# Reordering the opening of a decoder block: first tiles and first normalisation rows loaded in halves on both queues, first two value tiles multiplied in passes

## What is computed

```python
h = layer_norm(x, ln0_g, ln0_b)                 # per token, over 1024 features
proj = jnp.einsum('bsd,dn->bsn', h, w_in[i])     # 1024 x 7688 columns
(hg_q, hg_f, hg_i, hg_g, fx_q, ...) = jnp.split(proj, split_at, axis=-1)
...
v = i_lin.astype(jnp.float32)                    # hg_i, the values of the first mixer: 512 columns
```

## Time and profile before

| what | value |
|---|---|
| median of 3 runs | 1638.04 us (1636.09 to 1638.63) |
| the profiled execution's own time | 1637.65 us |
| its span, first to last instruction | 1635.8 us (1.85 us lie around it) |
| TensorE busy in the span | 1588.1 us, 97% |
| first transpose, first matmul of a product | 13.3 us, 17.99 us |
| second value tile's product done, third begins | 33.8 us |
| eight value tiles done | 71.2 us |

### The profile page before, as it was taken

One profiled execution on the slowest core, in us unless ns is written; L12 is line 12 of the kernel. 1 busy time (PEld: TensorE's weight loads), 2 busy tenths in 40 slices (PEclk: granted clock), 3 DMA queues, 4 the chain that ended last, 5 costly groups with the idle time before them and its releaser, 6 DMA issues.

```text
span 1635.8 us, 21111 instructions
## 1 busy us (share of the span) xinstructions
PE 1588.1 (97%) x7800; PEld 1325.1 (81%) x7800; DVE 1150.4 (70%) x1724; ACT 744.0 (45%) x1162; POOL 694.2 (42%) x487
## 2 busy tenths in 40 slices
PE   6999999999999999999999989999999999999996
PEld 4888888888888887888887868888888888888886
DVE  8558878437767668656336879986666579857977
ACT  3245454327888774511233644445444553433342
POOL 5222221522333145564443597765566323223334
PEclk9999999999999999999999999999999999999999
DMA  8211110101010143521333435554444598867672
GB/s 295 77 42 38 27 39 27 39 29 38 27 53 27 39 117 97 147 78 52 122 120 118 164 126 183 182 195 143 159 168 152 185 330 254 272 199 238 194 204 104
DMA packets 220693, 208.51 MB, mean 127 GB/s; under 512 B 9000, under 2 KB 190504, under 8 KB 218544
## 3 DMA queue, kind: packets, MB, share of 16 engines
q1 hardware_dynamic: 217424, 196.09, 38.7%
q10 hardware_dynamic: 3168, 11.08, 1.7%
HBM read 160.96 MB, written 46.17 MB: 127 GB/s over the span
## 4 chain that ended last, share of the span: by engine, by line
PE 83%; DVE 5%; ACT 4%; DMA 2%; POOL 2%; issue 2%; SPq 0%; DVEq 0%; ACTq 0%; POOLq 0%
PE dense L969 7%; PE dense L971 7%; PE dense L973 7%; PE dense L979 4%; PE dense L1315 3%; PE dense L1317 3%; PE dense L1316 3%; PE dense L1395 3%; PE dense L1396 3%; PE dense L1397 3%; PE mixA L1106 2%; PE dense L1047 2%; PE dense L1049 2%; PE dense L1048 2%; PE mixA L1315 2%
## 5 line engine op out<-in xcount | busy, mean ns | idle before, releaser
L969 PE MATMUL dense<-parts 128*128 128x512 f32 x528 | 183.3, 409 | 1.6 <-DVE page L2090 0.9
L943 POOL TENSOR_TENSOR parts<-page,parts 128x512 fp32r<-128x512 f32 x52 | 88.9, 1733 | 208.1 <-ACT parts L1909 208.1
L862 POOL TENSOR_TENSOR parts<-page,parts 128x512 fp32r<-128x512 f32 x108 | 156.3, 1469 | 44.9 <-ACT parts L1788 41.6
L971 PE MATMUL dense<-parts 128*128 128x512 f32 x528 | 174.0, 391 | 0.0
L973 PE MATMUL dense<-parts 128*128 128x512 f32 x528 | 173.3, 390 | 0.0
L854 POOL CAST parts<-page 128x1024 fp32r<-128x1024 f32 x43 | 49.3, 1145 | 287.4 <-PE dense L973 192.4
L905 POOL TENSOR_TENSOR page<-page 128x512 f32<-128x512 f32 x80 | 122.6, 1532 | 59.8 <-PE dense L1317 25.2
L913 POOL TENSOR_TENSOR parts<-page,parts 128x512 fp32r<-128x512 f32 x80 | 114.8, 1437 | 55.4 <-ACT parts L1835 50.6
L1919 ACT CAST parts<-page 128x1024 fp32r<-128x1024 f32 x56 | 58.8, 1055 | 142.8 <-DVE page L2614 123.2
L973 PEld LDWEIGHTS dense<-parts 128*128 128x128 f32 x528 | 99.1, 188 | 21.8
L971 PEld LDWEIGHTS dense<-parts 128*128 128x128 f32 x528 | 99.1, 188 | 21.0
(11 more groups left out here) (298 smaller groups left out, 4315.8 us busy)
## 6 DMA issues: line engine op xcount, KB each, us to landing
page<-in_w_ff SPq DMA_DIRECT2D x104, 512.0 KB, 6.0
page<-in_w_in SPq DMA_DIRECT2D x120, 256.0 KB, 3.2
page<-act_scratch SPq DMA_DIRECT2D x56, 512.0 KB, 5.7
act_scratch<-page SPq DMA_DIRECT2D x16, 1024.0 KB, 3.9
act_scratch<-page SPq DMA_DIRECT2D x16, 768.0 KB, 7.0
page<-in_w_o SPq DMA_DIRECT2D x32, 256.0 KB, 3.1
h_scratch<-page ACTq DMA_DIRECT2D x8, 512.0 KB, 3.5
page<-c_scratch SPq DMA_DIRECT2D x8, 512.0 KB, 5.0
```

The costliest lines, as they stand in the source:

```text
L862: ins = nc.gpsimd.tensor_tensor(R(lo, at, HALF), F(raw_page(c), at, HALF), R(hi, at, HALF).bitcast(F32), ALU.subtract)
L969: mm(o, whi, x_, start=first, stop=False)
L971: mm(o, whi, x_, start=False, stop=False)
```

## The change

The loads of tile 0, of the scale row, of the bias row and of tile 1 are cut into halves of 512 columns, one half on each queue (new semaphores or counts of idle ones for the second halves). SP then loads chunks 0 and 2, tiles 2 to 7, and the rest; ACT loads chunks 1 and 3 after its halves, and the identity between the scale's and the bias's. VectorE waits for scale and bias apart, and the order of tile 1 (begin, low part of the tile before, end) is used for tile 2 too. ScalarE makes tile 0's high part after the first chunk instead of the second, and postpones the first two stores of products. TensorE computes tiles 0 and 1 in passes: for tile 0 all eight high-by-high matmuls, all eight with the token's low part, then the low-weight ones in pieces between tile 1's passes, with the transposes of tiles 1 and 2 between them. The number of matmuls, transposes, copies and normalisation steps and of bytes is the same.

```diff
--- before.py
+++ after.py
@@ -391,6 +391,8 @@
         AFTER_LEVELS, AFTER_HEADS = HL * NHG, 2 * NHG
         g_done, g_hi, g_split, g_first, g_acc = lvl_done, ab_exp, ab_ready, ab_sub, pred_done
         g_psum, g_vsum, gt_in, gt_raw, gt_hi, gt_lo, g_sig = upd_done, st_ready, kt_done, sq_done, rms_done, rs_ready, o_done
+        x0_in, g0_in, b0_in, AFTER_X0, AFTER_B0 = c_stored, rows_in, pe_in, 16, 32
+        x1_in = sem("x1_in")
         heads_high = lambda hh: NHG + (3 * hh + 3 if hh < 2 else hh + 5)
 
 
@@ -610,14 +612,19 @@
                 m, k = {1: (1, 1), 2: (1, 2), 5: (2, 2), 6: (1, 1), 3: (1, 2), 7: (1, 1), 4: (2, 2)}[i]
                 sp.dma_start(as4(F(GSLOT[d], HALF, HALF)), block_of(m, k)).then_inc(gw_in[d], 16)
 
-            sp.dma_start(F(PG_X), x_t[0]).then_inc(x_in[0], 16)
+            sp.dma_start(F(PG_X, 0, HALF), x_t[0][:, 0:HALF]).then_inc(x_in[0], 16)
+            sp.dma_start(F(PG_G0, 0, HALF), row(ln0_g)[:, 0:HALF]).then_inc(g0_in, 16)
+            sp.dma_start(F(PG_B0, 0, HALF), row(ln0_b)[:, 0:HALF]).then_inc(b0_in, 16)
+            sp.dma_start(F(PG_X + 1, 0, HALF), x_t[1][:, 0:HALF]).then_inc(x_in[1], 16)
             for c in range(C_END):
+                if c in (1, 3):
+                    continue
                 if c == C_AB:
                     for w in range(GN):
                         load_gate(w)
                 load_chunk(c)
-                if c == 3:
-                    for t in range(4, TT):
+                if c == 2:
+                    for t in range(2, TT):
                         sp.dma_start(F(PG_X + t), x_t[t]).then_inc(x_in[t], 16)
                 if c == 5:
                     sp.dma_start(F(PG_T3, 0, P), c_causal).then_inc(consts_in, 16)
@@ -630,7 +637,7 @@
                 if c == 25:
                     sp.wait_ge(c_ready, 1)
                     sp.dma_start(c_scratch[:, :], F(PG_CROW)[0:NFX, :]).then_inc(c_stored, 16)
-                    sp.wait_ge(c_stored, 16)
+                    sp.wait_ge(c_stored, AFTER_X0 + 16)
                     load_negc(0)
                     load_negc(1)
                 if 27 <= c < 33:
@@ -1042,8 +1049,6 @@
                     wide = lambda base, k: R(base + k // 2, (k % 2) * HALF, HALF)
                 for k in range(KD):
                     xh, xl = R(XHI + k, t * P, P), R(XLO + k, t * P, P)
-                    if (name, t, k % 2) == ("vhg", 0, 0):
-                        pe.wait_ge(w0_split, k // 2 + 1)
                     mm(out1, xh, wide(WHI, k), start=k == 0, stop=False)
                     mm(out1, xh, wide(WLO, k), start=False, stop=False)
                     ins = mm(out1, xl, wide(WHI, k), start=False, stop=k == KD - 1)
@@ -1068,8 +1073,40 @@
                     ins = nc.tensor.transpose(dst[:, k * P:(k + 1) * P], F(PG_X + t, k * P, P), ident[:, :])
                 ins.then_inc(h_turned, 1)
 
+            def first_values(t, n, ks):
+
+                j = JOB["vhg", t]
+                out1 = dense[SET[j]][:, 0:HALF]
+                x_, base = (XHI, XLO, XHI)[n], (WHI, WHI, WLO)[n]
+                for k in ks:
+                    if t == 0 and n != 1 and k % 2 == 0:
+                        pe.wait_ge((w0_hi, None, w0_split)[n], k // 2 + 1)
+                    ins = mm(out1, R(x_ + k, t * P, P), R(base + k // 2, (k % 2) * HALF, HALF),
+                             start=n == 0 and k == 0, stop=n == 2 and k == KD - 1)
+                if n == 2 and ks[-1] == KD - 1:
+                    end(ins, j)
+
+            every, early, late = range(KD), range(KD - 2), range(KD - 2, KD)
             turn_tokens(0)
-            for t in range(TT):
+            begin(JOB["vhg", 0])
+            pe.wait_ge(h_hi, 1)
+            first_values(0, 0, every)
+            pe.wait_ge(h_split, 1)
+            first_values(0, 1, every)
+            first_values(0, 2, range(0, 2))
+            turn_tokens(1)
+            first_values(0, 2, range(2, 4))
+            begin(JOB["vhg", 1])
+            pe.wait_ge(h_hi, 2)
+            first_values(1, 0, every)
+            pe.wait_ge(h_split, 2)
+            first_values(1, 1, every)
+            first_values(0, 2, range(4, 6))
+            turn_tokens(2)
+            first_values(1, 2, early)
+            first_values(0, 2, late)
+            first_values(1, 2, late)
+            for t in range(2, TT):
                 pe.wait_ge(h_split, t + 1)
                 value_job("vhg", t, (2, turn_tokens))
 
@@ -1254,7 +1291,7 @@
                         pass
 
             def turn_embeddings():
-                pe.wait_ge(pe_in, 16)
+                pe.wait_ge(pe_in, AFTER_B0 + 16)
                 gate_evicted(GN - 1)
                 for k in range(2):
                     for t in range(TT):
@@ -1424,11 +1461,15 @@
             A = nc.scalar.activation
             count = [0]
             nc.scalar.preload_act_table_set("natural_log_exp_and_others")
-            act.dma_start(F(PG_G0), row(ln0_g)).then_inc(rows_in, 16)
-            act.dma_start(F(PG_B0), row(ln0_b)).then_inc(rows_in, 16)
+            act.dma_start(F(PG_X, HALF, HALF), x_t[0][:, HALF:]).then_inc(x0_in, 16)
+            act.dma_start(F(PG_G0, HALF, HALF), row(ln0_g)[:, HALF:]).then_inc(g0_in, 16)
             act.dma_start(ident[:, :], c_ident).then_inc(ident_in, 16)
-            for t in range(1, 4):
-                act.dma_start(F(PG_X + t), x_t[t]).then_inc(x_in[t], 16)
+            act.dma_start(F(PG_B0, HALF, HALF), row(ln0_b)[:, HALF:]).then_inc(b0_in, 16)
+            act.dma_start(F(PG_X + 1, HALF, HALF), x_t[1][:, HALF:]).then_inc(x1_in, 16)
+            for c in (1, 3):
+                for i in range(2):
+                    act.dma_start(F(PG_W0 + c, i * HALF, HALF), w_views["in"][:, 2 * c + i, C_HI:C_HI + HALF],
+                                  ).then_inc(w0_landed[c], 16)
 
             act.wait_ge(const_set, 4)
 
@@ -1462,10 +1503,16 @@
             for j in range(4):
                 act.wait_ge(w0_landed[j], 32)
                 nc.scalar.copy(R(WHI + j), F(PG_W0 + j)).then_inc(w0_hi, 1)
-                if j == 1:
+                if j == 0:
                     tokens_high(0)
                     rstd_estimate(1)
-            for t in range(1, TT + 1):
+            rstd_estimate(2)
+            tokens_high(1)
+            rstd_estimate(3)
+            tokens_high(2)
+            store_values(PG_VHG, "vhg", 0, 0)
+            store_values(PG_VHG, "vhg", 1, 0)
+            for t in range(3, TT + 1):
                 if t + 1 < TT:
                     rstd_estimate(t + 1)
                 if t < TT:
@@ -1613,7 +1660,7 @@
                     own_step(A(tmp, tmp, ACT.Exp, scale=-1.0))
                     A(tmp, tmp, ACT.Ln, bias=1.0).then_inc(c_log, 1)
                 if t == TT - 1:
-                    act.wait_ge(c_stored, 16)
+                    act.wait_ge(c_stored, AFTER_X0 + 16)
                 nc.scalar.copy(v_part(t, False, R), out_of("vfx", t)[:, 0:HG].rearrange(
                     "q (n c f) -> q n c f", n=NPAIR, c=2)).then_inc(v_ready, 1)
                 if t < 3:
@@ -1996,9 +2043,11 @@
             V.memset(mean_w[:, :], 1.0 / P).then_inc(const_set, 1)
             V.memset(eps[:, 0:1], LN_EPS).then_inc(const_set, 1)
             V.memset(eps[:, 1:2], RMS_EPS).then_inc(const_set, 1)
-            def norm_stats(src, i):
+            def norm_stats(src, i, second=None):
 
                 V.bn_stats(stats[:, i, 0, :], src[:, 0:HALF])
+                if second is not None:
+                    dve.wait_ge(*second)
                 then(V.bn_stats(stats[:, i, 1, :], src[:, HALF:]))
                 V.bn_aggr(mv[:, i, :], stats[:, i, :, :]).then_inc(var_ready, 1)
 
@@ -2039,7 +2088,7 @@
             all8 = lambda page: R(page, 0, KD * 1024).rearrange("q (k n) -> q k n", k=KD)
             def tokens_stats(t):
                 dve.wait_ge(x_in[t], 16)
-                norm_stats(F(PG_X + t), t % 2)
+                norm_stats(F(PG_X + t), t % 2, ((x0_in, 16), (x1_in, 16))[t] if t < 2 else None)
 
             def tokens_norm(t):
                 norm_apply(F(PG_X + t), F(PG_X + t), t % 2, F(PG_G0), F(PG_B0), t).then_inc(h_ready, 1)
@@ -2049,13 +2098,16 @@
                 low_part(all8(XLO), all8(XHI), (mixA, mixB)[t % 2], t).then_inc(h_split, 1)
 
             tokens_stats(0)
-            dve.wait_ge(rows_in, 32)
-            tokens_norm(0)
-            tokens_stats(1)
-            norm_begin(F(PG_X + 1), F(PG_X + 1), 1, F(PG_G0), 1)
-            tokens_low(0)
-            norm_end(F(PG_X + 1), 1, F(PG_B0), 1).then_inc(h_ready, 1)
-            for t in range(1, TT):
+            dve.wait_ge(g0_in, 32)
+            norm_begin(F(PG_X), F(PG_X), 0, F(PG_G0), 0)
+            dve.wait_ge(b0_in, 32)
+            norm_end(F(PG_X), 0, F(PG_B0), 0).then_inc(h_ready, 1)
+            for t in range(1, 3):
+                tokens_stats(t)
+                norm_begin(F(PG_X + t), F(PG_X + t), t % 2, F(PG_G0), t)
+                tokens_low(t - 1)
```

(2 more changed lines are left out.)

## The result

Over 20 runs each, the changed kernel takes **1640.35 us** (1638.98 to 1643.82), the kernel before 1636.64 us (1635.44 to 1638.63): ratio 1.0025, 95% interval 1.0018 to 1.0032, 3.7 us slower. The three runs shown ahead of the prediction were a little high for the kernel before (1638.04).

A forecast was written before the change was run, and what follows sets the result against it. VectorE's unbroken chain was taken to set tile 2's start; its delay of +1.1 us plus 1.6 for the clock's fall gave +2.7 us, on the profiled 1637.65 us 1640.3 us, range 1636.0 to 1643.0.

The forecast's parts named there:

- What bounds: Opening up to tile 2's product: VectorE's chain of 17.1 us without pause, not TensorE, sets its start at 33.8 us.
- Loads: Opening loads: x lands near 4.5 us, scale 6.0, bias 8.0; chunk 0 at 12.2 (bounds 11.6 and 13.2).
- the first pass: TensorE's first matmuls on tile 0: start at 14.3 us instead of 18.0, wait for ScalarE's copies, done at 18.6.
- Chunk 3: Weight loads: chunks 2 and 3 add 1 MB and land at 14.8 us, before ScalarE gets to them.
- The clock's rise: TensorE's opening: clock rises at 22.0 us (bounds 20.2 and 23.7), so ScalarE starts tile 1's high part at 23.6.
- VectorE's pause: Ahead of tile 1's low part: VectorE arrives at 21.3 us and waits 3.3 us for the high part, until 24.6.
- tile 2: Start of tile 2's product: 34.9 us, +1.1 us (bounds +0.2 and +2.0 by the clock).
- the idle stretch: TensorE ahead of tile 2: done at 31.9 us, then idle for 3.0 us.
- The clock's fall: After TensorE's idle stretch: matmuls in the low clock for 3.39 us cost 1.6 us (bounds 0 and 3.2).
- two low stretches: Clearly slower rival, ahead of tile 2: late rise plus one fall, or twice 3.39 us low; +3.6 to +4.3; chance 0.18.
- Nothing gives it back: From tile 2 on: TensorE stays the bound to 71 us and later waits shift along, so all +2.7 us remains.

The follow-up runs named there:

- the repairs: In the changed kernel, VectorE finishes tile 2's normalisation before tile 1's low part (1638.5 us), or tile 1's transposes directly follow the first pass (1638.31); both together 1636.53 us.
- the kernel before with an early clock: The kernel before with 28 added matmuls, results not read, ahead of tile 0's transposes: 1637.32 us, ratio 0.9998.
- the order alone: The kernel before with the new order of work on VectorE, ScalarE and TensorE and its old transfers: 1640.4 us, ratio 1.0018.
- the loads alone: The kernel before with the changed transfers only, all engines' order of work kept: 1640.76 us, ratio 1.0023.
- the first profile with the filled stretch: First of two profiles of the changed kernel with 11 added matmuls in TensorE's idle stretch ahead of tile 2: 1639.03 us, ratio 1.0012.
- early transposes, second: Second profile of the changed kernel with tile 1's transposes moved from behind tile 0's 18th matmul to behind its 8th: 1638.31 us, ratio 1.0005.
- After: Profile of the changed kernel, nothing else altered, taken with the 20 runs of the result: 1640.35 us, ratio 1.0025 to the kernel before.
- changed again: The changed kernel measured again, nothing altered, as base for its group, with a second profile: 1641.77 us, ratio 1.0017 to the kernel before.

## Why the prediction was right

The forecast was 1640.3 us and +2.7 by its sum; measured are 1640.35 and +3.7. The absolute number is closer than the sum deserves, and that is luck: the profiled execution that it starts from was 1.0 us above the median of 20 runs. Step by step:

- **What bounds.** VectorE's chain sets tile 2's start: shown by the repairs, alone and together, and by the kernel before with an early clock.
- **Loads.** x by 4.1 us (4.5 forecast), scale by 6.1 (6.0). The bias row was mis-sized: complete at 10.1, not 8.0. Its halves, 256 KB each, took 6.2 us on SP's queue (issued at 1.65) and 7.9 on ACT's (issued at 2.15):

```profile
page<-in_ln_b SPq DMA_DIRECT2D x1, 256.0 KB, 6.2
...
page<-in_x SPq DMA_DIRECT2D x1, 256.0 KB, 7.4
page<-in_ln_b ACTq DMA_DIRECT2D x1, 256.0 KB, 7.9
```

  From 5 to 10 us the queues moved 306 GB/s, where I had taken the 357 of the kernel before, whose transfers there were partly of 4 KB rows. The step that failed is "at 0.36 MB per us x lands near 4.5 us, scale 6.0, bias 8.0", in its last term. Tile 0's transposes ended at 14.05, and ScalarE waited 0.45 us for them with chunk 0 already copied; with the 0.4 us by which chunk 0 was late (12.59, forecast 12.2), the first pass started at 15.15 instead of 14.3.
- **Chunk 3** was forecast for 14.8 us and landed at 17.9, inside the first pass: behind chunk 2, SP's queue carries 4 KB rows against ACT's 2 KB ones and takes the larger part. From 10 to 12.6 us, with 2 KB rows on both, each moved 0.53 MB; from 12.6 to 17.9 us SP's moved 1.54 MB and ACT's 0.60. The first pass ended near 19.4 instead of 18.6.
- **The clock's rise** was forecast for 22.0 (20.2 to 23.7). It came at 18.8 and 20.9 in the two profiles of this kernel, and between 18.6 and 24.2 in the eight other kernels that add nothing ahead of tile 0. My bounds, 20.2 and 23.7, were too narrow. That it came early in these two cancels the two errors before it, which is luck too: ScalarE starts the high part at 22.90 and 23.68, for 23.6.
- **VectorE's pause** was 2.30 and 2.25 us, for 3.3: VectorE came to that low part at 21.7 and 22.5 us, for 21.3; **tile 2** at 34.42 and 35.25, for 34.9; **the idle stretch** 2.91 and 2.97, for 3.0.
- **The clock's fall.** 1.6 us in one profile, 2.8 in the other (4.26 - 1.44), for 1.6. This is the term that was too small in the mean: I gave two low stretches 0.18 together with the late rise, and one of two profiles has them, with no late rise. That is my reading of the difference between +2.7 and +3.7; two profiles can't show it, and the profiles of the order alone and of the loads alone leave 1.3 and 2.2 us of their medians' losses unexplained.
- **Nothing gives it back:** so up to 835 us; behind that the runs wander by as much as the effect.

The Trainium skill, Trainium Kernel Development and Optimization, section Key Constraints, held as far as the halves go: x and scale came sooner with less ahead of them, and both queues together moved no more than before (306 and 405 GB/s, for 357 and 409). The Trainium skill, TensorE: Matmul & The Clock Gate, Part 1, says that the rise comes at another matmul from run to run. These runs now show it: 18.8 against 20.9 us in one program.

## What to carry to other kernels

When an engine is 97% busy, look for the last place where it waited, and for the engine that has no pause up to there: an earlier start elsewhere is worth nothing until that chain moves (here TensorE's first product started 2.8 us earlier and tile 2's 0.6 us later). Before work is put between an engine's product and its consumer (here ten matmuls ahead of the transposes), ask who stands idle behind the consumer. And price an idle stretch of TensorE of 3 us at more than itself: in the two profiles here the low clock added 1.6 and 2.8 us to the work that followed. And carry every engine through a change of the loads: GpSimd, for which TensorE never waited in the opening of the kernel before, held it up with the loads alone.

## What the runs showed that I had not expected

- The same wait does not always lower the clock. Ahead of the same matmul (L1242 in the kernel before) TensorE waits 3.2 us near 640 us; the clock fell in it or behind it in every profile but one. In the first profile with the filled stretch it stayed high there:

```profile
641.80 0.50 PE L1281 MATMUL dense<-parts 128*128 128x512 f32 x1 [3.22 <-POOL parts L835]
...
1357.02 0.80 PE L1434 MATMUL dense<-parts 128*128 128x512 f32 x1 [2.53 <-DVE parts L2593]
```

  and fell at the second of these two waits instead, of 2.53 us. Waits of 2.49 (order of work alone), 1.61 (early transposes, second) and 1.4 us left it high. A fall came up to 1.45 us after work had resumed.
- VectorE's pass over two SBUF operands takes 1.27 us if it starts just ahead of GpSimd's subtraction and 2.20 if it starts just behind it (above): 0.9 us of this pass hang on 0.25 us of timing. *After* and *changed again* differ in the same way: 1.27 us with GpSimd 0.20 us behind, 2.12 with GpSimd 0.23 ahead, and the low part of tile 0 starts at 15.20 and 15.64.
- Of two halves issued within half a microsecond of each other on the two queues, the one on ACT's queue was complete 2 us later (7.85 and 10.05 us). With the identity behind it instead of ahead it was still complete only at 9.9. The reason stays open.
